# RWKV state stored with zeros for 128-row products, and the recurrence, branch, modulation and retention products in another order

## The reference, cut to what matters

```python
def hybrid_layer(x, ...):
    h = _rms(x) * norm1_g
    aq, ak, av, rw, rq, rk, rv, rg, gates = _split(h @ w_in, IN_SIZES)
    o_a = sliding_window_attention(aq, ak, av, attn_sinks) @ w_attn_o
    o_b = rwkv7_time_mix(rw, ...) @ w_rwkv_o
    o_c = retention(rq, rk, rv, rg) @ w_ret_o
    g = jax.nn.sigmoid(gates).reshape(B, T, N_BRANCH, D)
    mixed = g[:, :, 0] * o_a + g[:, :, 1] * o_b + g[:, :, 2] * o_c
    x = x + mixed @ w_out
    h2 = _rms(x) * norm2_g
    return x + (jax.nn.silu(h2 @ w_ffn_gate) * (h2 @ w_ffn_up)) @ w_ffn_down

def step(S, inp):                       # the recurrence of rwkv7_time_mix, 8 heads of 64
    r_t, w_t, k_t, v_t, a_t, b_t = inp
    Sa = jnp.einsum('bhvk,bhk->bhv', S, a_t)
    S = S * w_t[:, :, None, :] + Sa[..., None] * b_t[:, :, None, :] + v_t[..., None] * k_t[:, :, None, :]
    return S, jnp.einsum('bhvk,bhk->bhv', S, r_t)
```

## Time and profile before

| | us |
|---|---|
| median of 3 runs | 2488.67 (2487.16 to 2494.41) |
| the profiled execution | 2485.83 |
| its span, first to last instruction | 2484.0 |
| TensorE busy with matmuls | 1993.3 |
| VectorE busy | 854.3 |
| ScalarE busy | 443.4 |
| mean granted TensorE clock | 0.899 |

### The profile page before, as it was taken

The page is one execution under the profiler, slowest core; times in us unless marked ns, Lnnn a source line. Parts: engine busy times, 40 slices in busy tenths (PEclk is TensorE's granted clock), DMA queues, the critical chain, the costliest instruction groups (busy, mean ns, idle before and its releaser), DMA issues.

```text
span 2484.0 us, 29513 instructions
## 1 busy us (share of the span) xinstructions
PE 1993.3 (80%) x12744; PEld 1400.2 (56%) x12744; DVE 854.3 (34%) x1186; ACT 443.4 (18%) x429; POOL 33.6 (1%) x19
## 2 busy tenths in 40 slices
PE   7999999999999999999889776656566555556565
PEld 7987779999988779999567472111111111111111
DVE  6744448556656347654246431000000000000001
ACT  3422012333522112332232001000000000000000
POOL 0000010000000010000000000000000000000000
PEclk9999989999999999999989787778778888887877
DMA  6432534656432624557322036999999999999996
GB/s 238 154 136 102 195 112 160 204 160 204 169 139 102 226 106 136 170 165 202 121 78 74 0 158 259 418 417 418 418 417 418 418 418 417 418 417 418 418 417 256
DMA packets 230872, 613.00 MB, mean 247 GB/s; under 512 B 11196, under 2 KB 106684, under 8 KB 197180
## 3 DMA queue, kind: packets, MB, share of 16 engines
q1 hardware_dynamic: 228704, 602.19, 63.8%
q10 hardware_dynamic: 2076, 9.45, 1.1%
HBM read 610.55 MB, written 1.05 MB: 246 GB/s over the span
## 4 chain that ended last, share of the span: by engine, by line
PE 55%; DMA 24%; SPq 12%; DVE 6%; ACT 2%; issue 1%; ACTq 0%; DVEq 0%; PEldq 0%
SPq L1164 12%; PE PS L1269 10%; DMA work<-in_w_up 8%; PE PS L1325 7%; PE PS L1318 7%; PE PS L1320 7%; DMA work<-in_w_gate 7%; DMA work<-in_w_down 7%; PE PS L564 6%; PE PS L746 2%; DMA ring<-in_w_out 1%; PE PS L760 1%; PE PS L1251 1%; PE PS L1491 1%; DVE ring_low L1931 1%
## 5 line engine op out<-in xcount | busy, mean ns | idle before, releaser
L746 PE MATMUL PS<-ring,proj 128*32 128x512 f32 x1280 | 195.7, 741 | 130.9 <-DMA ring<-in_w_up 66.8
L760 PE MATMUL PS<-work,proj 128*32 128x512 f32 x768 | 135.8, 844 | 108.6 <-DMA work<-in_w_down 108.6
L746 PE MATMUL PS<-work,proj 128*32 128x512 f32 x768 | 132.7, 828 | 98.6 <-DMA work<-in_w_up 64.5
L1269 PE MATMUL PS<-hT,ring 128*128 128x256 f32 x896 | 202.0, 385 | 0.0
L1126 DVE TENSOR_TENSOR proj<-proj,PS 128x512 f32<-128x512 f32 x16 | 11.0, 687 | 550.9 <-PE PS L746 550.9
L746 PEld LDWEIGHTS PS<-ring,proj 128*32 128x32 f32 x1280 | 38.2, 123 | 272.6 <-DMA ring<-in_w_up 109.2
L1269 PEld LDWEIGHTS PS<-hT,ring 128*128 128x128 f32 x896 | 170.7, 193 | 25.3 <-issue 1.7
L1931 DVE TENSOR_TENSOR ring_low<-ring,high_f 128x4096 fp32r<-128x4096 f32 (+1 forms) x38 | 146.8, 3864 | 58.3 <-ACT high_f L1747 58.3
L1747 ACT ACTIVATE high_f<-ring 128x4096 fp32r<-128x4096 f32 (+1 forms) x38 | 120.8, 3179 | 218.4 <-PE PS L1325 179.3
L1318 PE MATMUL PS<-xh_f,high_f 128*128 128x256 f32 x640 | 153.6, 280 | 0.3 <-DVE xh_f L1940 0.2
L564 PE MATMUL PS<-hT,ring 128*128 128x256 f32 (+1 forms) x640 | 146.7, 390 | 8.0 <-DVE hT L918 8.0
(11 more groups left out here) (446 smaller groups left out, 3140.5 us busy)
## 6 DMA issues: line engine op xcount, KB each, us to landing
ring<-in_w_gate SPq DMA_DIRECT2D x96, 1024.0 KB, 19.7
work<-in_w_down SPq DMA_DIRECT2D x96, 1024.0 KB, 19.6
ring<-in_w_in SPq DMA_DIRECT2D x74, 1024.0 KB, 7.3
work<-in_w_up SPq DMA_DIRECT2D x64, 1024.0 KB, 25.3
ring<-in_w_up SPq DMA_DIRECT2D x64, 1024.0 KB, 25.2
work<-in_w_gate SPq DMA_DIRECT2D x32, 1024.0 KB, 23.5
ring<-in_w_down SPq DMA_DIRECT2D x32, 1024.0 KB, 25.3
ring<-in_w_ada SPq DMA_DIRECT2D x24, 1024.0 KB, 6.8
```

What stands on the lines that cost most here:

```text
L746: mm = nt.matmul(PS[32 * j:32 * j + 32, 2 + n // 4, :], XSE[:, k, :], w[:, F_E * kk + 512 * j:F_E * kk + 512 * (j + 1)], start=(k == 0), s ...
L760: mm = nt.matmul(PS[32 * g:32 * g + 32, 5, :], HTE[:, P * c + 32 * d:P * c + 32 * (d + 1)], w[:, D * c + 512 * dh:D * c + 512 * (dh + 1)], ...
L1269: mm = nt.matmul(PS[:, bank(l, q), T * b:T * (b + 1)], weight(b, k), moving(k), start=(k == 0), stop=(k == kn - 1))
```

## The change

- `ST` has the two heads of a block side by side, `[P, HB, 2, HD]`, each with the other head's 64 partitions zero. L1513 and L1535 then use all 128 rows, where before they used the 64 of their head. POOL writes the zeros once per layer, and the state copy is two instructions.
- `ada(0)` goes ahead of the levels, the others move one place forward; blocks are renumbered to match.
- Branch 0's four products move: the second from inside chunk 0 to behind its state product, the third into chunk 1 behind u, the fourth from chunk 1 to behind the retention products.
- The transposes of V go into chunk 1; the copies of them on ScalarE too.
- Scores: heads in the order 0, 2, 3, 1, 4, 6, 7, 5, the first two ahead of the wait for y. The norm uses PSUM banks 6 and 7 in place of 0 and 1, the retention output banks 2 and 3 in place of 6 and 7.
- VectorE's `low_weights(l, S_OUT)` goes behind the square of the retention output and the fourth product's take-out.

The ring's slots, SP's order and ScalarE's order around `high_weights(l, S_OUT)` are not in the diff.

```diff
-Q_ADA = [30, 31, 32, 33, 35, 37]
+Q_ADA = [30, 31, 32, 33, 34, 36]
-Q_MIX = [[34, 36, 39, 40], [41, 42, 43, 44], [45, 46, 47, 48]]
+Q_MIX = [[35, 37, 39, 40], [41, 42, 43, 44], [45, 46, 47, 48]]
+SCORE_HEADS = [0, 2, 3, 1, 4, 6, 7, 5]
...
+                pool.memset(ST, 0.0).then_inc(gm_zero, 1)
                 pool.memset(w_(9216, 3072), 0.0).then_inc(gm_zero, 1)
...
             def rwkv_levels(l):
+                ada(l, 0)
...
-                        ada(l, (lev - BASE_LEVEL) * 2 + pair // 2)
+                        ada(l, (lev - BASE_LEVEL) * 2 + pair // 2 + 1)
...
                     if t:
-                        nt.matmul(out, AR[hrow(h), h // 2, t, 0, :], ST[hrow(h), h // 2, :], start=True, stop=False)
+                        nt.matmul(out, AR[:, h // 2, t, 0, :], ST[:, h // 2, h % 2, :], start=True, stop=False)
                     mm = nt.matmul(out, GM[:, h, P:2 * P], VTOK[:, t, HD * h:HD * (h + 1)], start=(t == 0), stop=True)
                 mm.then_inc(rhs_ready, 1)
-                mix(l, 0, 2 * t, 2 * t + 1)
                 if t == 0:
-                    ada(l, 4)
-                else:
-                    pe.wait_ge(rot_out, 1)
+                    mix(l, 0, 0, 1)
                 rotate((B_RQ, B_RK)[t])
...
-                mix(l, 0, 2 * t + 1, 2 * t + 2)
                 if t == 0:
                     ada(l, 5)
+                else:
+                    mix(l, 0, 2, 3)
+                    values_by_token()
...
                     if t:
-                        mm = nt.matmul(out, ST[hrow(h), h // 2, :], AR[hrow(h), h // 2, t, 1, :], start=False, stop=True)
+                        mm = nt.matmul(out, ST[:, h // 2, h % 2, :], AR[:, h // 2, t, 1, :], start=False, stop=True)
...
                     mm.then_inc(s_ready, 1)
+                    mix(l, 0, 1, 2)
...
+                pe.wait_ge(rot_out, 2)
+                scores(0, 2)
                 pe.wait_ge(y_out, 2)
-                pe.wait_ge(dve_taken, taken_at(l, Q_MIX[0][-1]))
-                head_sums(0, Y, ln_ss)
-                for t in range(TT):
-                    for b in range(HB):
-                        mm = nt.transpose(PS[:, 6 + t, P * b:P * (b + 1)], proj[:, B_RV + b, P * t:P * (t + 1)], ident)
-                mm.then_inc(vr_ready, 1)
-                pe.wait_ge(rot_out, 2)
-                scores(0, 4)
+                pe.wait_ge(vr_out, 2)
+                head_sums(6, Y, ln_ss)
+                scores(2, 4)
...
                 mm.then_inc(oc_psum, 1)
+                mix(l, 0, 3, 4)
                 mix(l, 1, 0, 2)
...
                 nv.tensor_tensor(Y, Y, r, ALU.add).then_inc(ob_ready, 1)
-                low_weights(l, S_OUT)
...
                 nv.tensor_tensor(XR, o, o, ALU.mult).then_inc(oc_sq, 1)
+                mix(l, 0, 3, 4)
+                low_weights(l, S_OUT)
                 mix(l, 1, 0, 1)
```

More of the change, by code:

```diff
@@ L310, in build @@
         VTOK, BKT = w_(13312, TT, 512), w_(14336, 2, 512)
[L311 removed]
+        RHS, U, ST = w_(2048, HEADS, HD), w_(2560, HEADS, HD), w_(15872, HB, 2, HD)
         MID, SC, MIDE = small[:, 0:8].rearrange("p (a b) -> p a b", b=TT), small[:, 8:12], small[:, 12:16]
@@ L320, in build @@
         GATED = w_(6144, HB, T)
-        VRET, XR = w_(13312, TT, 512), w_(14336, HB, T)
+        VRET, XR = w_(14336, TT, 512), w_(14336, HB, T)
         SQ, STD, RSTD = w_(5120, KD, T), w_(0, T), w_(256, T)
@@ L1502, in rotate, with values_by_token @@
                 mm.then_inc(rot_ready, 1)
+            def values_by_token():
+                for t in range(TT):
+                    for b in range(HB):
+                        mm = nt.transpose(PS[:, 6 + t, P * b:P * (b + 1)], proj[:, B_RV + b, P * t:P * (t + 1)], ident)
+                mm.then_inc(vr_ready, 1)
             def rwkv_chunk(l, t):
@@ L1589, in scores @@
                 def scores(lo, hi):
-                    for h in range(lo, hi):
+                    for i in range(lo, hi):
+                        h = SCORE_HEADS[i]
                         o, b, bk = hrow(h), h // 2, 2 + h % 2 + 2 * (h // 2 % 2)
-                        if h >= 4:
-                            pe.wait_ge(rs_out, h - 3)
+                        if i >= 4:
+                            pe.wait_ge(rs_out, i - 3)
                         nt.matmul(PS[:, bk, 0:T], proj[o, B_RK + b, 0:P], proj[o, B_RQ + b, :], start=True, stop=True)
@@ L1801, in rwkv_chunk @@
                 na.activation(U[:, :, :].rearrange("p a b -> p (a b)"), PS[:, 2, :], ACT.Copy).then_inc(u_out, 1)
+                if t:
+                    act.wait_ge(vr_ready, 1)
+                    for n in range(TT):
+                        na.activation(VRET[:, n, :], PS[:, 6 + n, :], ACT.Copy).then_inc(vr_out, 1)
                 act.wait_ge(y_ready, t + 1)
@@ L1805, in rwkv_norm @@
             def rwkv_norm():
-                act.wait_ge(vr_ready, 1)
-                for t in range(TT):
-                    na.activation(VRET[:, t, :], PS[:, 6 + t, :], ACT.Copy).then_inc(vr_out, 1)
                 act.wait_ge(ln_ss, 2)
-                na.activation(LN_STAT, PS[:, 0, 0:4 * HB], ACT.Sqrt, bias=lnxc, scale=1.0 / HD).then_inc(ln_std, 1)
+                na.activation(LN_STAT, PS[:, 6, 0:4 * HB], ACT.Sqrt, bias=lnxc, scale=1.0 / HD).then_inc(ln_std, 1)
             def attention(l):
@@ L2085, in rwkv_grams @@
             def rwkv_grams(t):
-                dve.wait_ge(gm_zero, 1)
+                dve.wait_ge(gm_zero, 2)
                 if t:
@@ L2109, in rwkv_levels @@
             def rwkv_levels(l):
+                ada_rows(l, 0)
                 for lev in range(BASE_LEVEL, LEVELS):
@@ L2129, in rwkv_chunk @@
                     rwkv_levels(l)
+                    mix(l, 0, 0, 1)
                 else:
                     ada_columns(l)
-                mix(l, 0, 2 * t, 2 * t + 1)
-                if t == 0:
-                    ada_rows(l, 4)
                 rotation(l, t)
-                mix(l, 0, 2 * t + 1, 2 * t + 2)
                 if t == 0:
@@ L2139, in rwkv_chunk @@
                     dve.wait_ge(s_ready, 1)
-                    nv.tensor_tensor(ST, banks(5, 1, HB, HD), SC.unsqueeze(2).broadcast_to([P, HB, HD]), ALU.mult).then_inc(st_ready, 1)
+                    for n in range(2):
+                        o = hrow(n)
+                        ins = nv.tensor_tensor(ST[o, :, n, :], PS[o, 5, 0:HB * HD].rearrange("p (a b) -> p a b", b=HD),
+                                               SC[o, :].unsqueeze(2).broadcast_to([HD, HB, HD]), ALU.mult)
+                    ins.then_inc(st_ready, 1)
+                    mix(l, 0, 1, 2)
+                else:
+                    mix(l, 0, 2, 3)
             def attention(l):
@@ L2208, in scores @@
                 def scores(lo, hi):
-                    for h in range(lo, hi):
-                        dve.wait_ge(rs_ready, h + 1)
+                    for i in range(lo, hi):
+                        h = SCORE_HEADS[i]
+                        dve.wait_ge(rs_ready, i + 1)
                         nv.tensor_tensor(SM[:, h, :], PS[:, 2 + h % 2 + 2 * (h // 2 % 2), 0:3 * P], DEC[:, h, :], ALU.mult).then_inc(rs_out, 1)
```

19 lines of the change are left out of this document (10 added, 9 removed).

## The result

The changed kernel is slower. Medians of the runs of both kernels on one chip: 2516.19 us (2513.67 to 2522.48) against 2488.15 us (2487.16 to 2494.41), a ratio of 1.0111 with a 95% interval of 1.0085 to 1.0138. The profiled execution took 2518.49 us, of which 2516.7 is span; that of before took 2485.83.

The account below looks back on a forecast made before the run. TensorE's own order was taken as the bound. Gains of 21.2 us against 46.5 us for the late slot release gave +25.3: 2511.1 us, or 2514 against the median; range 2502 to 2527, slower at 0.91.

Parts of the forecast that it names:

- the two reasons named: Behind mix(0,3,4), TensorE waits for w_rwkv_o's late transfer, then for VectorE, held up through ScalarE's wait for w_out.
- ada(0) into the wait: Ahead of the second chunk, ada(0) fills TensorE's 1.2 us wait at L1479: gain 1.2 us per layer.
- right sides, second chunk: With 128 rows throughout, the 32 records take 3.84 us: gain 3.99 us in layer 0, 3.45 in layer 1.
- product behind them: The mix product behind the second chunk's right sides runs at full clock: gain 2.69 and 1.65 us, or 0.
- y: Second chunk's y products take 2.70 us at 128 rows and scores(0,2) fill the wait: gain 5.58 us per layer.
- retention: Between y and the first rwkv_o product, transposes, scores and head order cost 2.1 us per layer, bounds 1.0 and 3.0.
- ring: Late release of w_attn_o's slot by mix(0,3,4) lengthens the stretch to the first ret_o product by 23.1 and 23.4 us.
- net: All gains and costs over both layers together: the kernel gets 25.3 us slower.
- the two waits: TensorE's new idle rows: near 8 us a layer for w_rwkv_o's transfer, and again near 14 us for VectorE.
- the clock of 1.00 through both stages: Sign expected: TensorE stays at full clock through the second chunk's right sides and y products.
- rival 3: Wait behind mix(0,3,4) is cheaper, no clock lost, VectorE before POOL: near M + 40, 7 us less, 2507; chance 0.15.
- Rival 2: Clock falls in the second chunk all the same, after grams paced by VectorE: 7.0 us lost, 2521; chance 0.20.

Follow-up runs that it names:

- experiment 1: Changed kernel with mix(0,3,4) put back inside the second chunk, all else kept: 2472.08 us, 0.9929 of the kernel before.
- experiment 2: Changed kernel with ScalarE's high_weights(S_OUT) behind the retention copy and VectorE's low_weights(S_OUT) behind the fourth w_rwkv_o product: 2488.66 us, 0.9998 of before.
- experiment 7: Changed kernel with mix(0,3,4) on TensorE moved between scores(2,4) and head_columns: 2489.38 us, 0.9999 of the kernel before.
- experiment 3: Changed kernel with score heads ordered 0, 3, 2, 1, 4, 7, 6, 5, neighbours in opposite halves: 2510.70 us, 1.0081 of before.
- experiment 6: Changed kernel with mix(0,3,4) back in the second chunk and neighbouring score heads in opposite halves: 2475.98 us, 0.9946 of before.
- experiment 8: Changed kernel with mix(0,3,4) back, opposite halves, ScalarE's retention() ahead of high_weights, VectorE's low_weights behind the fourth w_rwkv_o product: 2461.70 us, 0.9888 of before.
- experiment 5: Kernel before with only the state's zeros added (ST twice as wide, products over 128 rows), old order kept: 2480.57 us, 0.9965 of before.
- experiment 9: Kernel before with the state's zeros, ScalarE's retention() ahead of high_weights, VectorE's low_weights behind the fourth w_rwkv_o product: 2460.78 us, 0.9895 of before.
- experiment 10: Kernel before with only ScalarE's retention() ahead of high_weights and VectorE's low_weights behind the fourth w_rwkv_o product, no zeros: 2481.16 us, 0.9970 of before.
- experiment 4: Changed kernel with the state's products over 64 rows again, zeros written but not read: 2535.85 us, 1.0190 of before.

## Why the prediction was right, and where it was off

The sign and the mechanism were right: idle time of TensorE behind mix(0,3,4), in two pieces, for the two reasons named. Term by term, from the two profiled executions:

| term, us | predicted, layer 0 / 1 | measured |
|---|---|---|
| ada(0) into the wait | 1.2 / 1.2 | 1.2 / 1.2 |
| right sides, second chunk | 3.99 / 3.45 | 2.0 / 3.5 |
| product behind them | 2.69 / 1.65 | 1.4 / 1.7 |
| y | 5.58 / 5.58 | 5.2 / 5.2 |
| retention | -2.1 / -2.1 | -6.4 / -6.0 |
| ring | -23.1 / -23.4 | -19.7 / -23.0 |
| net | -11.7 / -13.6 | -16.3 / -17.5 |

The net is the shift of the first w_ret_o product against the grams of its layer; some 0.1 of layer 1 is in no term. Of what was to show it, the two waits, ScalarE's wait of over 20 us, SP's late issue and the 128 rows came; the clock of 1.00 through both stages did not in layer 0, and y took 3.0 for 2.7. Four things in it:

*The ring was 3.8 us too dear.* The measured M + 40.2 is rival 3's number (M + 40) in layer 0, M + 42.3 nearly the forecast's (42.7) in layer 1. The second product came at M + 25.1 and 26.2 for 27.2, because w_out was there at M + 18.7, for 19.4, and VectorE went ahead of POOL (L2247 took 1.23 us for the 2.4 that I took). Half clock behind the idle stretches was there, which rival 3 did without: the second product, taken as 5.5 us, took 5.67 and in layer 1 6.70, and the first one 5.57, for 3.6 at full clock; the latter is hidden, since TensorE was idle again behind it. Experiments 1, 2 and 7 show each half of the mechanism by itself.

*The retention was the mis-sized step*: "Cost 2.1 per layer, bounds 1.0 and 3.0", measured 6.4 and 6.0. I priced the new order of heads at 0.6, as if only the overlap between neighbours' ends were lost, and for scores(4,8) alone. Eight heads' scores took 3.5 us before and take 7.4. And the half clock, of which I said that it might give 0.6 back, grew from 3 us to 10. Experiment 3 shows both to hang on the order of heads: with it undone the retention is 4.5 us shorter in either layer, and the 1.9 that remain in layer 0 are what I had counted for the transposes and the two heads (0.96 and 1.1).

*Rival 2 came true in layer 0 only*: 0.50 from 307 to 313, 1.00 in layer 1. The zeros took the alternation away and the clock fell all the same there. It cost 3.3 us (2.0 on the right sides, 1.3 behind) of the 7.0 priced for two layers. What lowers it stays open. The alternation is not needed for it: with the zeros in the changed order the right sides meet the low clock in layer 0 of all seven kernels (the changed one and experiments 1, 2, 3, 6, 7 and 8), and in layer 1 of experiments 3 and 7 (5.21 and 5.57 us for 3.62). It is not without effect either: in the old order they stay at full clock in all four layers with the zeros (experiments 5 and 9) and fall in all four without (before and experiment 10). And since layer 1 goes both ways with one and the same order, the order of the products does not decide it alone.

*The total is closer than the terms, in part by luck.* The gains were 12.2 us too high (21.2 for 9.0), the ring 3.8 too dear, so the shift came to 33.8 where 25.3 stood: 8.5 us off. Of these the end of the trace shows 7.4 (it rose by 32.7). The median of the runs rose by only 28.0, since the two traced executions lie on opposite sides of their medians; that, and no part of the reasoning, brings 2514 to within 2.2 us of 2516.2.

One reading was off without consequence: TensorE is at nine tenths up to slice 19, not 18.

What I did not see at all is that the kernel before was already close to this limit, and that the zeros without any reordering would lose more than half of their gain to it (experiment 5). "Every microsecond taken off TensorE's queue moves the end" holds only until ScalarE's copy meets w_out: in the trace of before, the copy followed the retention products by some 2 us already, the wait of 2.0 at L1369.

## What to carry to other kernels

A product that is the last reader of a ring slot is also the start of every load behind it: before moving it, write down its end, the transfers in order, and who on each in-order queue stands behind the last of them; here 3.7 us of work carried 44 us. A wait for a late transfer belongs behind all work of its engine that does not need it: putting both engines' work on w_out there was worth 6 us in the kernel before, 27.5 in the changed one, and it is what lets a gain upstream show. When a saving comes out as half of what the operations lost, look for the first wait that has grown; the work may have been saved in full.

## What the runs showed of the hardware

*Two heads of one half.* Products of 64 rows in the same half took 0.76 us a head at full clock, in opposite halves 0.43.

*The length of the low stretch in the retention follows the order of heads.* Windows of 2 us over layer 0: with neighbours in one half the clock is at 0.50 for 7 to 10 us (the changed kernel, experiments 1, 2, 4 and 7), with opposite halves for some 3 us (before, experiments 3, 5, 6, 8, 9 and 10). In experiment 7 it falls with TensorE busy without a gap for the 18 us before. Two pairs among them differ in nothing but the order of heads (the changed kernel and experiment 3, experiments 1 and 6). This is seen in one profiled execution of each of twelve kernels, not explained.

*The clock also falls where the code is the same.* In the kernel before, the way from the first grams of a layer to those of its second chunk takes 51.9 us in both layers, at 1.00. In experiments 9 and 10, with the same products there, layer 0 takes 55.3, at 0.62 from 279 to 288 us, and in experiment 5 53.6. A difference of 3 us between two traced executions can be this alone.

*VectorE and POOL.* L1942 takes 5.97 us in the changed kernel (370.75, above) where the same form took 4.43: POOL's L1227, begun at 369.05, ends at 372.43, 1.68 us into it. The Trainium skill (SBUF — State Buffer, SBUF: two separate sides) says that a VectorE instruction with two SBUF inputs and a GpSimd one that reads SBUF exclude each other, and that the one that starts first keeps the other out until it is through. The trace agrees: L1942, with two SBUF inputs, is longer by 1.54 us; L2247 began 0.04 us ahead of L1227 and was not delayed; and L2270, with one of its inputs in PSUM, took 0.68 us beside L1227, no longer than elsewhere.

*Alternating row counts.* With 64 and 128 rows in turn the groups of two records of the right sides in experiment 4 come every 0.36 us at full clock (304.72, 305.08), with 128 rows throughout every 0.225 (305.49 to 305.94 in the changed kernel). The Trainium skill (TensorEngine Tiling (Array Packing), Key Properties) says that a change of the tiling mode drains TensorE; the trace agrees, with some 0.13 us for each change in the right sides. The figure is not a general one: in the y products a head with its two changes takes 0.94 us (experiment 4, as before), with 128 rows throughout 0.38 (3.04 for eight heads), 0.28 for each change.
